# Modulation weights read by TensorE as plain fp32 in four column groups, with the first norm and projection begun on half of the chunks

## What is computed

```python
silu_c = jax.nn.silu(c)
silu_cc = jax.nn.silu(c_ctx)
for i in range(2):
    mod_x = silu_c @ w_mod[i] + b_mod[i]        # w_mod[i]: 1024 x 3072
    mod_c = silu_cc @ w_mod[i] + b_mod[i]
    sh_x, sc_x, g_x = split(mod_x, 3)           # shift, scale, gate: 1024 each
    sh_c, sc_c, g_c = split(mod_c, 3)
    hx = rms_norm(x, norm_g[i]) * (1 + sc_x) + sh_x
    hc = rms_norm(ctx, norm_g[i]) * (1 + sc_c) + sh_c
    yx, yc = mixer(i, hx, hc)   # i = 0: a_w_in, attention, a_w_out; i = 1: b_w_in, attention, b_w_out
    x = x + g_x * yx
    ctx = ctx + g_c * yc        # not in the last layer
```

## Time and profile before

| | |
|---|---|
| median of 3 runs | 2140.45 us (2140.16 to 2144.67) |
| the profiled execution, its own time | 2143.55 us |
| its span | 2141.7 us |
| PE busy | 1987.0 us (93%) |
| DVE, ACT, GpSimd busy | 1497.5, 1250.7, 66.2 us |
| mean granted PE clock | 0.967 |
| from 0 to 513 us | the two layers up to the second attention: all that the diff touches |

### The profile page before, as it was taken

One profiled execution on the slowest core, in us unless ns is written; L12 is line 12 of the kernel. 1 busy time (PEld: TensorE's weight loads), 2 busy tenths in 40 slices (PEclk: granted clock), 3 DMA queues, 4 the chain that ended last, 5 costly groups with the idle time before them and its releaser, 6 DMA issues.

```text
span 2141.7 us, 28471 instructions
## 1 busy us (share of the span) xinstructions
PE 1987.0 (93%) x10785; PEld 1635.4 (76%) x10785; DVE 1497.5 (70%) x1530; ACT 1250.7 (58%) x1345; POOL 66.2 (3%) x51
## 2 busy tenths in 40 slices
PE   5889998999789789999867999999999999999997
PEld 3667567787478579998756888888888888888886
DVE  5574765425755645455657889898898989889885
ACT  5334763425535643434535777777777777777774
POOL 0110000001200000000020000000000000000000
PEclk9999999999989899999988999999999999999999
DMA  8244102535435445554337999999999999999993
GB/s 305 99 137 150 67 21 79 197 99 96 83 115 154 127 133 181 179 194 142 119 138 243 376 344 366 357 353 377 339 367 344 365 358 352 377 337 371 341 367 134
DMA packets 275584, 496.89 MB, mean 232 GB/s; under 512 B 25940, under 2 KB 52984, under 8 KB 275496
## 3 DMA queue, kind: packets, MB, share of 16 engines
q1 hardware_dynamic: 273104, 489.72, 66.6%
q0 software_dynamic: 944, 3.31, 0.5%
q10 hardware_dynamic: 1448, 2.66, 0.3%
HBM read 494.58 MB, written 1.07 MB: 231 GB/s over the span
## 4 chain that ended last, share of the span: by engine, by line
issue 49%; PE 37%; DVE 5%; ACT 4%; DMA 2%; SPq 2%; POOL 1%; DVEq 0%; POOLq 0%; ACTq 0%; PEldq 0%
PE bank L1664 10%; PE bank L1665 10%; PE bank L1666 10%; ACT w_hi L680 1%; PE bank L1805 1%; PE bank L1794 1%; PE bank L1819 1%; DVE w_lo L1042 1%; SPq L581 1%; PE bank L1718 1%; DMA bias_b<-in_b_rpb 1%; DMA first_raw_q<-in_w_mod 1%; SPq L566 1%; PE bank L1856 1%; PE bank L1885 1%
## 5 line engine op out<-in xcount | busy, mean ns | idle before, releaser
L1042 DVE TENSOR_TENSOR w_lo<-raw,w_hi 128x2048 fp32r<-128x2048 f32 x117 | 266.9, 2290 | 289.7 <-ACT w_hi L680 289.5
L1461 DVE TENSOR_TENSOR w_lo<-raw,w_hi 128x2048 fp32r<-128x2048 f32 x165 | 373.5, 2287 | 58.0 <-ACT w_hi L954 58.0
L1461 DVE TENSOR_TENSOR w_lo_x<-raw_x,w_hi_x 128x2048 fp32r<-128x2048 f32 x165 | 376.2, 2290 | 41.9 <-ACT w_hi_x L954 40.8
L954 ACT ACTIVATE w_hi_x<-raw_x 128x2048 fp32r<-128x2048 f32 x168 | 323.2, 1924 | 129.1 <-PE bank L1666 129.1
L954 ACT ACTIVATE w_hi<-raw 128x2048 fp32r<-128x2048 f32 x168 | 322.3, 1919 | 44.9 <-PE bank L1666 44.4
L680 ACT ACTIVATE w_hi<-raw 128x2048 fp32r<-128x2048 f32 x117 | 222.5, 1909 | 197.9 <-PE bank L1666 193.8
L1664 PE MATMUL bank<-h_hi,w_hi 128*128 128x256 f32 (+1 forms) x864 | 261.0, 302 | 9.9 <-DVE w_lo L1042 6.2
L1665 PE MATMUL bank<-h_lo,w_hi 128*128 128x256 f32 (+1 forms) x864 | 258.5, 299 | 0.0
L1666 PE MATMUL bank<-h_hi,w_lo 128*128 128x256 f32 (+1 forms) x864 | 258.4, 299 | 0.0
L1664 PE MATMUL bank<-w_hi,xe_hi 128*128 128x512 f32 x612 | 243.0, 397 | 1.4 <-DVE xe_lo L1512 1.4
L1666 PE MATMUL bank<-w_hi,xe_lo 128*128 128x512 f32 x612 | 238.8, 390 | 0.0
(11 more groups left out here) (290 smaller groups left out, 3279.7 us busy)
## 6 DMA issues: line engine op xcount, KB each, us to landing
raw<-in_e_w SPq DMA_DIRECT2D x168, 1024.0 KB, 7.0
raw_x<-in_e_w SPq DMA_DIRECT2D x168, 1024.0 KB, 7.4
raw<-in_w SPq DMA_DIRECT2D x33, 1024.0 KB, 5.3
raw<-in_w_qkv SPq DMA_DIRECT2D x24, 1024.0 KB, 5.1
raw<-in_w_mod SPq DMA_DIRECT2D x19, 1024.0 KB, 5.3
raw<-in_b_w_in SPq DMA_DIRECT2D x16, 1024.0 KB, 5.7
raw<-in_a_w_in SPq DMA_DIRECT2D x9, 1024.0 KB, 5.1
raw<-in_w_o SPq DMA_DIRECT2D x8, 1024.0 KB, 5.2
```

The lines of the kernel that those rows point to most:

```text
L954: nc.scalar.activation(ring6(w_hi, w_hi_x, n, 1)[:, 0, :], ring6(raw, raw_x, n, 1)[:, 0, :], ACT.Copy).then_inc(x_hi_ready, 1)
L1042: nc.vector.tensor_tensor(w_lo[:, m % NSPLIT, :], raw_unit(m), w_hi[:, m % NSPLIT, :].bitcast(F32), ALU.subtract).then_inc(lo_ready, 1)
L1461: nc.vector.tensor_tensor(ring6(w_lo, w_lo_x, n, 1)[:, 0, :], ring6(raw, raw_x, n, 1)[:, 0, :], ring6(w_hi, w_hi_x, n, 1)[:, 0, :].bitcast ...
```

## The change

Modulation units are no longer split: PE reads them from `raw` as plain fp32, with the stationary operand `silu_c` (128 x 4). The four chunks of a unit go to four column groups of the array: output partitions 0, 32, 64 and 96. Two blocks share one accumulation: one writes rows 0 and 1 of each group and the other rows 2 and 3, since `silu_c` is zero in the other two columns. So there are six accumulations (`MODS`) where there were twelve. The copy out and the turning take all 128 partitions; the turning matmul adds the four groups up.

A slot of `raw` that held a modulation unit is free when PE has used it (`wait_used` in `load_unit`). The units' order changes: the first four are shift and scale of chunks 0 to 3; then half 0 of the first `a_in` block; the other four of layer 0; half 1; and the rest in pairs behind `a_in` 0 to 3, behind `a_out` 0, inside `a_out` 1 (between its halves), and behind `b_in` 0 and 1. PE's norm of chunks 4 to 7, and half 1 of the first block, come after half 0. GpSimd makes `w_lo` of the first projection unit. x and ctx are loaded from SP's queue behind the first two units. "Two beyond" in `split` now counts projection units alone (`beyond`).

```diff
+MODS = [(0, (0, 2)), (0, (1, 3)), (0, (4, 5)), (1, (0, 2)), (1, (1, 3)), (1, (4, 5))]
...
+    mods_after = {("a_in", 0): [2, 0], ("a_in", 1): [2, 1], ("a_in", 2): [3, 0], ("a_in", 3): [3, 1],
+                  ("b_in", 0): [5, 0], ("b_in", 1): [5, 1]}
+    mods_between = {("a_in", 0): [1, 0, 1], ("a_out", 1): [4, 1]}
+    mods_after["a_out", 0] = [4, 0]
...
     def columns_and_mods(name, w):
         for cb in range(w.shape[1] // 512):
+            one_unit(name, w, cb, 0)
+            if (name, cb) in mods_between:
+                mod_columns(*mods_between[name, cb])
+            one_unit(name, w, cb, 1)
+            if (name, cb) in mods_after:
+                mod_columns(*mods_after[name, cb])
+
+    mod_columns(0, 0, 1)
     columns_and_mods("a_in", a_w_in)
...
+    def beyond(m, n):
+
+        return whole_units[min(splits_before(m + 1) + n, len(whole_units)) - 1] + 1
...
                 if n >= NRAW + NFIRST:
 
-                    sp.wait_ge(lo_ready, raw_unit_before(n) + 1)
+                    m = raw_unit_before(n)
+                    if m in whole_units:
+                        sp.wait_ge(lo_ready, splits_before(m + 1))
+                    else:
+                        wait_used(sp, m)
...
             for n in range(NS):
+                if n == 2:
+                    for tokens, src in ((slice(0, TT), A["x"]), (slice(TT, 2 * TT), A["ctx"])):
+                        sp.dma_start(xs[:, tokens, :], src[0].rearrange("(t p) d -> p t d", p=P)).then_inc(sem("x_landed"), 16)
...
-            split(1)
             act.wait_ge(sem("vec_t_ready"), 1)
...
+            for s in range(2):
+                nc.scalar.activation(silu_c[:, :, s, 2 * s:2 * s + 2].rearrange("p c w -> p w c"),
...
             def linear(name, blocks, evac, after=None):
 
                 for pos in range(blocks):
-                    split(step_unit(name, pos, 1) + 3)
+                    split(beyond(step_unit(name, pos, 1), 2))
                     for i in range(blocks_of[name][pos]):
                         evacuate(name, pos, i, evac)
...
+            norm_squares("n0", 4, lambda t: (sem("x_landed"), 32))
+            keep_mod_row(0)
+            split(unit_at["a_in", 0, 0] + 1)
+
+            def second_half():
+                keep_mod_row(1)
+                split(unit_at["a_in", 0, 1] + 1)
+
+            norm("n0", 4, None, None, second_half)
...
             attention_by_two("a")
-            split(at["a_out"] + 4)
-            split(at["b_in"] + 2)
+            split(beyond(last_unit["a_out"], 2))
+            keep_mod_row(4)
...
                 for cb in range(2):
-                    split(at[name] + 4 if name in ("o0", "o1") else at[name] + 2 * cb + 4)
+                    split(at[name] + 4 if name in ("o0", "o1") else beyond(unit_at[name, cb, 1], 2))
...
+            def second_half():
+                dve.wait_ge(lo_ready, 1)
+                split(unit_at["a_in", 0, 1] + 1)
+                add_mod_bias(1)
+                gains(0, 1)
...
+            pool.wait_ge(hi_ready, 1)
+            nc.gpsimd.tensor_tensor(w_lo[:, split_slot(m), :], raw_unit(m), w_hi[:, split_slot(m), :].bitcast(F32), ALU.subtract)\
+              .then_inc(lo_ready, 1)
...
+            def mod_unit(q, s, half):
+
+                l, blocks = MODS[q]
+                m = unit_at[f"mod{l}", blocks[s], half]
+                pe.wait_ge(*raw_landed(m))
...
                 for c in range(4):
+                    ins = nc.tensor.matmul(mod_bank(q)[32 * c:32 * c + 4, :], silu_c[:, 4 * half + c, s, :], w[:, c, :],
+                                           start=s + half == 0, stop=s + half == 2)
                 ins.then_inc(w_used, 1)
...
+                pe.wait_ge(sem("mod_row_ready"), q + 1)
                 for i in range(4):
+                    ins = nc.tensor.matmul(mod_bank(q)[:, 4 * i:4 * i + 4], mod_row[:, i * P:(i + 1) * P], spread, start=True, stop=True)
                 ins.then_inc(sem("mod_turned"), 1)
...
+            mod_units(0, 0, 1)
+            turn_mod(0)
...
+            norm_chunks("n0", 4, range(CH - 1))
+            pe.wait_ge(*reached("n0", "h_lo", CH // 2))
+            for i in range(4):
+                half_group("a_in", 0, 0, i, ("rows", i))
+                if i == 1:
+                    mod_units(*mods_between["a_in", 0])
+                if i == 2:
+                    turn_mod(1)
+            pe.wait_ge(sem("mod_ready"), 2)
+            norm_chunks("n0", 4, [CH - 1])
+            for i in range(4):
+                half_group("a_in", 0, 1, i, ("rows", i), None, "n0" if i == 0 else None)
...
+            def mods_in_a_out(cb, half, i):
+                if cb == 1 and (half, i) == (0, 3):
+                    mod_units(*mods_between["a_out", 1])
+                if cb == 1 and (half, i) == (1, 0):
+                    turn_mod(4)
+
+            linear("a_out", 2, lambda cb: rows(4), lambda cb: mods_done("a_out", cb), between=mods_in_a_out)
```

More of the change, by code:

```diff
@@ L537, in qk_slot, with mod_bank, mod_row_of @@
             return z_a[:, 4 + j % 4, :]
[L539 to L545, removed]
+        def mod_bank(q):
+            return bank[7 if q else 3]
+        def mod_row_of(q):
+            return gate_row if MODS[q][1] == (4, 5) else mod_row
+        rows_turned = [q for q in range(len(MODS)) if MODS[q][1] != (4, 5)]
         def group_ends(st):
@@ L851, in mods @@
             def mods(name, cb):
-                for l, c in mods_after.get((name, cb), []):
-                    for half in range(2):
-                        split(unit_at[f"mod{l}", c, half] + 3)
-                    keep_mod_row(l, c)
+                if mods_after.get((name, cb), [0, 0])[1] == 1:
+                    keep_mod_row(mods_after[name, cb][0])
             def turn_a(cb):
@@ L1370, in _ @@
             for cb in range(8):
-                split(unit_at["b_in", cb, 1] + 3)
+                split(beyond(unit_at["b_in", cb, 1], 2))
             def gate_bx(p, b, o):
@@ L1692, in mod_unit, with mod_units, turn_mod @@
                 ins.then_inc(w_used, 1)
-            def turn_mod(l, cb):
-                pe.wait_ge(sem("mod_row_ready"), 6 * l + cb + 1)
+            def mod_units(q, *which):
+                for s in which:
+                    for half in range(2):
+                        mod_unit(q, s, half)
+            def turn_mod(q):
+                pe.wait_ge(sem("mod_row_ready"), q + 1)
                 for i in range(4):
-                    ins = nc.tensor.matmul(mod_bank(l, cb)[:, 2 * i:2 * i + 2], mod_row_of(cb)[:, i * P:(i + 1) * P], spread[:, ::P],
-                                           start=True, stop=True)
+                    ins = nc.tensor.matmul(mod_bank(q)[:, 4 * i:4 * i + 4], mod_row[:, i * P:(i + 1) * P], spread, start=True, stop=True)
@@ L1710, in _, with norm_chunks @@
             pe.wait_ge(sem("t5_copied"), 1)
-            def norm(st, tiles):
-                pe.wait_ge(*reached(st, "diag", tiles))
-                for c in range(CH):
+            def norm_chunks(st, tiles, chunks):
+                for c in chunks:
                     if c >= 4:
                         pe.wait_ge(*reached(st, "h_lo", c - 3))
+                    if (st, c) == ("n1", 3):
+                        pe.wait_ge(sem("mod_ready"), 4)
                     for t in range(tiles):
@@ L1748, in half_group, with linear @@
                     ins.then_inc(w_used, 1)
-            def linear(name, blocks, forms, after=None, st=None):
-                for cb in range(blocks):
+            def linear(name, blocks, forms, after=None, st=None, between=None, begin=0):
+                for cb in range(begin, blocks):
                     for half in range(2):
```

288 lines of the change are left out of this document (150 added, 138 removed).

## The result

The changed kernel takes 2173.36 us (median of 4 runs, 2170.14 to 2173.83); the kernel before took 2140.30 beside it (4 runs, 2140.14 to 2144.67). The ratio is 1.0146, with a 95% interval of 1.0129 to 1.0164: the change makes the kernel 33 us slower, against 40 in the forecast. The profiled execution took 2170.14 us, with a span of 2167.7, of which PE is busy 1959.5 (90%).

The account below looks back on a forecast made before the run. PE was taken to bound the touched part. Start -18, `a_in` +15.3, attention -2, `a_out` +31.6 and `b_in` +13 sum to +40: 2183.5 on the profiled 2143.6, stated as 2180 us against the median, range 2155 to 2212.

Parts of the forecast that it names:

- the slots don't bind: Rival: held-back unit returns so fast that ACT and DVE are not kept from the banks; 2097 us, chance 0.06.
- the pair's row: Earlier trace's two-column-group row, 16 instructions in 1.02 us; basis for taking 0.95 us per modulation unit on PE.
- The 6 us that the prediction adds to its sum: Modulation units on PE: at the skill's 2.38 times, about 1.4 us each, the sum would rise about 6 us.
- its own rival: Rival: the column groups don't overlap, 2.5 us more per modulation unit; 2220 us, chance 0.08.
- The start: Up to the end of `a_in` block 0: ends at 65.5 against 83.5, 18 us won, give or take 4.
- costs nothing: First norm: GpSimd's subtraction, 4.8 us from 26.5 to 31.3, runs beside the norm and so costs nothing.
- The 2.9 us granted for a falling clock: At the start, up to 2.9 us allowed for a clock that falls in the thin stretch before block 0 ends.
- the expectation above: Undoing the half-chunk start in the changed kernel: 8 us longer, 2181; 8 of the start's 17 us from half-chunks.
- The pauses in `a_in`: PE's waits behind `a_in` blocks 0 to 4 change by +3.9, +4.9, +6.0, +6.8 and -13.2 us.
- four losses of 2.7 us: `a_in`: half clock after four pauses loses 10.8 us, against 3.9 before: +6.9 us.
- The attention: First attention starts on a warm clock, its row before showing 0.95 granted: -2 us.
- `a_out` and `b_in`: `a_out` +31.6 us, from waits till 16.6 and of 6.7 among others; `b_in` +13, 6.6 for each of blocks 0 and 1.

Follow-up runs that it names:

- the first experiment: Changed kernel with ACT and DVE emptying the banks before splitting the second unit beyond, in `a_in` and `b_in` only: 2128.94 us, ratio 0.9945.
- the two kernels in which the slots no longer hold back ACT and DVE: Changed kernel with banks emptied first in `a_in`, `b_in` and `a_out`: 2105.34 us; the same with the last four modulation units behind `b_in` 2 and 3: 2099.90 us.
- One group: Changed kernel with all four matmuls of a modulation unit in the same column group, as one accumulating chain: 2216.40 us, ratio 1.0351.
- the best version with the whole norm: Changed kernel with all order changes and last four modulation units behind `b_in` 2 and 3, but the half-chunk start undone: 2105.22 us, ratio 0.9844.

## Why the prediction was right, point by point

**The direction and the mechanism.** The forecast was 2180 us and slower, with 0.90; it is 2173.36. The new waits stand where they were said to stand, for the reason that was given, and the first experiment shows that the reason is the cause: with the banks emptied first, the waits on evacuations are gone and 44 us come back. The priced rival of the other side, "the slots don't bind", gave 2097; the two kernels in which the slots no longer hold back ACT and DVE take 2105 and 2100.

**The modulation unit.** Taken at 0.95 us from the pair's row. Sixteen instructions, two units, took 1.87 us (319.96 in the chain), 0.94 each. One group took 13.3 us for 31 distances, 0.43 each, 3.43 a unit, as the earlier trace rows gave (3.4). Line 1750 has 192 instructions in all, 24 units, so there were 20 behind the first four, not 22 as the prediction has it; the sum did not use that number. The overlap is 3.43 to 0.94, 3.7 times for four groups. The price came out right from thinner evidence than it seemed: of the two lines in the earlier trace rows only the first has two column groups (128*64); the score pairs of the second hold 64*128, half of the rows and all of the columns. The Trainium skill, TensorE: Matmul & The Clock Gate, section on measured speedup, has 2.38 times for three column groups and nothing for four; by its row a unit would have cost about 1.4 us, an estimate, and the trace does not agree: 0.94. The 6 us that the prediction adds to its sum for such a unit is low beside its own rival: there 2.5 us a unit make 40, so 0.45 would make 7.

**The start.** -18 predicted, -17.4 measured, but not by the same parts. The norm began at 25.27 (25.5 predicted). Its first half took 10.4 us, to 35.69, instead of 7.9: here the step failed that GpSimd's subtraction "costs nothing" beside the norm (last section). The 2.9 us granted for a falling clock were not needed: block 0 ran at full clock (1.00), though the norm's first half had 0.84. The allowance and this loss are of about the same size, so the end of block 0 (66.09 against 65.5) came out right partly by luck. And the share of the two halves of the change I had wrong, in the expectation above: 3 to 5.5 us come from the half-chunk start, not 8.

**The pauses in `a_in`.** The five pauses are +7.3 against +8.4. Predicted 8.7, 15.3, 14.2, 13.7 and 1.2 us; measured, from the ends and starts in the table, 8.9, 15.1, 13.5, 13.8 and 0.7.

**The clock in `a_in`: the term that was mis-sized.** I took four losses of 2.7 us, 10.8 together. Against a block at full clock (22.05), blocks 1 to 4 lost 2.1, 1.3, 1.65 and 1.6: 6.7. The granted clock around the first two pauses, and the step in the chain at which PE's matmuls go from 0.43 to 0.23 us:

```profile
71.00:75.00 4.00, 0.04 (x1) 0.70 1.05 395
75.00:78.50 3.50, 3.50 (x8) 0.50 0.60 219
78.50:99.00 20.50, 20.50 (x89) 0.98 0.16 52
104.00:112.00 8.00, 0.00 (x0) 0.67 0.76 285
114.30:118.00 3.70, 3.70 (x13) 0.64 0.22 28
```

```profile
79.14 0.43 PE bank L1728
79.57 0.23 PE bank L1729
```

The granted clock falls within the pauses (0.70 and 0.67) and is half (0.50, 1.2 GHz) when the work begins. But in the row that I priced by the earlier trace rows it stayed there for 5.2 us of the block; here for about 4.5 (75.0 to 79.5), and behind the second pause for 2.7 (0.64 over 3.7 us). I had multiplied one row by four. Counted from PE's first instruction behind the pause, half clock lasted about 4.5, 3.5, 4.3 and 6.0 us (from 74.96, 113.44, 150.28 and 186.08), against 6.0 in the kernel before (from 120.01); behind the fourth pause, 2.4 of the 6.0 fell on turns ahead of the block. Why the clock came back at different times these rows do not tell. That is 4.2 of the 7 us by which the forecast was too high.

**The attention.** -2 taken, -4.1 measured: 81.51 us at 1.00 instead of 84.01 at 0.95, and the rest in the pause behind it (3.2 us instead of 4.8). Together with the clock in `a_in` this makes 6.3 of the 7 us.

**`a_out` and `b_in`.** +31.7 against +31.6, and +12.9 against +13. Within `a_out`: 16.6 to the first matmul of block 1 (16.6 predicted), and 7.6 before the turn (6.7 predicted; the row was there 12.3 us after the modulation matmuls began at 350.37, not 11.3). That the sums agree to 0.1 us is luck. In `a_out` that wait and the turn at half clock (1.87 us in the chain, 1.05 taken) cost 1.7 us more than forecast, and the 46.0 us of before already held about 2 us of half clock (0.95 granted) that the sum did not take off. In `b_in` the pause behind block 1 grew by 4.7 us (9.3 after 4.6), not 4.0, as the load landed 5.96 us after its issue and not 5.1; against that, the second of the two clock losses was 1.3 and not 2.6 (111.66 against 110.37).

## What to carry to other kernels

When a unit of work moves from one engine to another, look at whose buffer it now holds, and for how long: here a cheap unit (0.94 us) held a slot until the end of a block, and the loss came from what was queued behind the split of that slot's next unit. "Prepare two ahead, then empty the banks" is safe only as long as both units ahead were already there; with a slot that PE frees late, empty first. Moving one or two lines in the order of one engine (42 of the 44 us in `a_in` and `b_in` came from ScalarE's alone) shows in which engine a loss sits, and gives it back.

## What the runs showed of the hardware beside that

**VectorE's subtraction stood still beside GpSimd's.** The timeline of the changed kernel's first norm, 25 to 35 us (start, length, engine, what, and in brackets the idle time before it and what ended it):

```profile
25.98 4.53 POOL L1681 TENSOR_TENSOR w_lo<-first_raw_q,w_hi 128x2048 fp32r<-128x2048 f32 x1 [1.78 <-ACT w_hi L721]
26.51 1.00 DVE L1184 TENSOR_SCALAR work<-bank,gain,mod 128x256 f32<-128x256 f32 x2 [0.97 <-PE bank L1780]
28.20 2.87 DVE L1168 TENSOR_TENSOR h_lo<-work,h_hi 128x512 fp32r<-128x512 f32 x1 [0.69 <-ACT h_hi L781]
...
34.60 0.69 DVE L1168 TENSOR_TENSOR h_lo<-work,h_hi 128x512 fp32r<-128x512 f32 x1 [1.04 <-ACT h_hi L781]
```

The subtraction `h_lo` takes 0.69 us in the earlier trace rows and in the last line, and 2.87 here; it ends at 31.07, 0.56 after GpSimd's ends at 30.51. DVE's scaling at 26.51, which reads its tile from a bank, kept its usual half microsecond each (0.99 for two in the earlier trace rows). So the 2.2 us fell on the one DVE instruction with two tiles in SBUF. It repeats in all nine other profiles of kernels with this subtraction on GpSimd. In eight of them `h_lo` takes 2.54 to 3.12 us and ends 0.54 to 0.56 after GpSimd's. In the best version with the whole norm it is the first gain instruction, 4.41 us for 128 by 4 numbers, where the shortest took 0.15; it ends with GpSimd's (41.27 and 41.25). The Trainium skill, SBUF — State Buffer, section on the two separate sides, says that the two engines share a pair of ports as an exclusive lock, which such an instruction of VectorE takes against GpSimd's, and that the loser fully blocks; the traces agree with it, 2.87 against 0.69. That I had called GpSimd's 4.5 us hidden because another engine ran beside it is the mistake to learn from.

**The last of three loads.** Three megabytes issued within 1.3 us: the last landed 9.29 us after its issue (322.27 in the chain). The first of three issued together landed after 5.28 (67.12). So what stood before the held-back load in the same queue added 4.0 us to its own 5.3.
